# Expert stage of a two-block transformer kernel: tokens of an expert group gathered once, pair by pair after

## The reference

```python
def hier_moe(h, w_grp, b_grp, w_exp, b_exp, w1, w3, w2):
    """Top-1 group routing then top-2 expert routing within the group; SwiGLU experts."""
    ...
    grp_p = jax.nn.softmax(tf @ w_grp.astype(f32) + b_grp.astype(f32), axis=-1)
    g_idx = jnp.argmax(grp_p, axis=-1)
    ...
    top_p, top_i = lax.top_k(jax.nn.softmax(in_grp, axis=-1), TOP_K)
    ...
        hid = jax.nn.silu(xb @ w1[e]) * (xb @ w3[e])
        return (hid @ w2[e]) * w_b[:, None].astype(t.dtype)
```

## Time and profile before

| | us |
|---|---|
| median of 3 runs (lowest to highest) | 2380.0 (2376.22 to 2380.07) |
| the profiled execution | 2379.42 |
| its span in the trace | 2377.5 |
| TensorE busy in it | 2333.4 (98%) |
| VectorE (DVE) busy | 970.1 (41%) |
| ScalarE (ACT) busy | 430.5 (18%) |

### The profile page before, as it was taken

How to read it: one execution, slowest core, us unless ns; L and a number is a source line. 1 busy time by engine, 2 the same in 40 slices (tenths; PEclk the granted TensorE clock), 3 DMA queues, 4 the chain that set the end, 5 groups by cost and what they waited for, 6 DMA issues and landing times.

```text
span 2377.5 us, 24384 instructions
## 1 busy us (share of the span) xinstructions
PE 2333.4 (98%) x10310; PEld 1388.3 (58%) x10310; DVE 970.1 (41%) x1839; ACT 430.5 (18%) x971; POOL 75.3 (3%) x130
## 2 busy tenths in 40 slices
PE   8999999999999999999899999999999999999998
PEld 5568548875586448786444444435878644444443
DVE  3567656677576544462222221222355321122112
ACT  3310003365100021220111111111122021111111
POOL 2000000010100000000000000000000000000000
PEclk9999999999999999999999999999999999999999
DMA  7379625354796342256899999993325589999995
GB/s 283 127 308 394 234 89 190 131 202 165 283 406 258 129 160 102 93 216 244 338 427 428 427 428 428 426 411 123 138 92 228 229 359 427 427 428 428 428 426 238
DMA packets 57434, 671.53 MB, mean 282 GB/s; under 512 B 7312, under 2 KB 7600, under 8 KB 18528
## 3 DMA queue, kind: packets, MB, share of 16 engines
q1 hardware_dynamic: 50160, 649.45, 67.1%
q0 software_dynamic: 7152, 20.39, 2.5%
HBM read 666.56 MB, written 3.26 MB: 282 GB/s over the span
## 4 chain that ended last, share of the span: by engine, by line
PE 93%; DVE 3%; DMA 3%; ACT 0%; issue 0%; POOL 0%; SPq 0%; DVEq 0%; POOLq 0%; ACTq 0%
PE ps L101 91%; DMA ring<-in_mlp_w 1%; DVE arena L117 1%; DVE arena L114 1%; DMA arena<-ssm_rows 1%; PE ps L323 1%; PE ps L2465 1%; DMA ring<-in_attn_w_in 1%; PE ps L2447 0%; PE ps L593 0%; DVE X L117 0%; PE ps L1722 0%; DVE arena L110 0%; ACT arena L106 0%; PE ps L1184 0%
## 5 line engine op out<-in xcount | busy, mean ns | idle before, releaser
L101 PE MATMUL ps<-arena 128*64 128x512 f32 (+5 forms) x3656 | 864.2, 462 | 5.8 <-DVE arena L117 3.7
L101 PEld LDWEIGHTS ps<-arena 128*128 128x128 f32 (+2 forms) x3656 | 418.0, 168 | 370.0 <-issue 351.8
L101 PE MATMUL ps<-XTGB,ring 128*128 128x256 f32 x2544 | 565.7, 381 | 5.0 <-DMA ring<-in_mlp_w 5.0
L101 PE MATMUL ps<-ring,arena 128*64 128x512 f32 (+1 forms) x1808 | 555.0, 593 | 0.0
L101 PEld LDWEIGHTS ps<-XTGB,ring 128*128 128x128 f32 x2544 | 479.9, 190 | 78.9 <-issue 7.8
L101 PEld LDWEIGHTS ps<-ring,arena 128*64 128x64 f32 (+1 forms) x1808 | 195.7, 149 | 284.9 <-issue 282.5
L117 DVE TENSOR_TENSOR arena<-ps,arena 128x512 f32<-128x512 f32 (+4 forms) x166 | 96.0, 613 | 364.8 <-PE ps L101 351.4
L101 PE MATMUL ps<-ring,XTGB 128*128 128x512 f32 (+3 forms) x568 | 226.6, 557 | 1.6 <-DMA ring<-in_attn_w_in 1.0
L101 PE MATMUL ps<-XTGB,arena 128*64 128x512 f32 (+1 forms) x576 | 197.6, 499 | 0.0
L121 ACT COPY arena<-ps 128x512 f32<-128x512 f32 (+2 forms) x169 | 75.7, 469 | 601.1 <-PE ps L101 279.5
L117 DVE TENSOR_TENSOR arena<-arena,ps 128x512 f32<-128x512 f32 x36 | 24.8, 688 | 388.6 <-PE ps L101 388.6
(11 more groups left out here) (140 smaller groups left out, 924.0 us busy)
## 6 DMA issues: line engine op xcount, KB each, us to landing
ring<-in_exp_w SPq DMA_DIRECT2D x88, 2048.0 KB, 19.6
arena<-in_exp_w SPq DMA_DIRECT2D x80, 2048.0 KB, 18.7
ring<-in_mlp_w SPq DMA_DIRECT2D x26, 2048.0 KB, 8.9
XTGB<-in_exp_w SPq DMA_DIRECT2D x20, 2048.0 KB, 19.4
ring<-in_ada_w SPq DMA_DIRECT2D x19, 2048.0 KB, 10.1
ring<-in_ssm_w_in SPq DMA_DIRECT2D x12, 2048.0 KB, 7.8
ring<-in_w_in SPq DMA_DIRECT2D x12, 2048.0 KB, 7.8
ring<-in_gate_w SPq DMA_DIRECT2D x12, 2048.0 KB, 7.8
```

What stands on the lines that cost most here:

```text
L101: return self.e.matmul(o, lhsT=lhsT, rhs=rhs, start=start, stop=stop, skip_group_check=True)
```

## The change

The first thing that the stage does now is to give each token a place in its group: a small pair of matmuls (`grank`) on the group mask, then `gcode` and `pg`, a matrix of 256 tokens x 128 places of the group. `group_rows(g)` brings the group's tokens together as up to 128 rows `xr` with four matmuls of 512 columns. `group_cols` does the same with the group's eight columns of `code` and of `wc`; they go to `cs`. From then on a pair's psel is one tile of 128x128 (group places x pair places), the gather reads xr with one matmul for each column block, `turn_w` is one transpose, and `combine` is one matmul for each half of the columns, which adds the four pairs of a group up in two PSUM banks (`ys`) held for the whole stage. After a group's last pair, DVE multiplies the sum by the gate (`group_sum`), `scatter(g)` brings it back to the tokens with four matmuls through `pgt` (pg turned), and DVE adds the four results to X (`to_tokens`). `rows_out` is a plain copy. psel has one buffer instead of two. The flag is also set if a group has more than 128 tokens.

Where the new steps stand on TensorE: grank, group_rows(0), rank, group_cols for code, then the first gather; `turn_g` between exp_w1 and exp_w3 of the second pair of a group; group_rows and both group_cols of the next group between exp_w1 and exp_w3 of the fourth; scatter of the group before ahead of the outer product of the first. The copies of xr are on ACT.

```diff
-            ps = bank(pe, "rank", l, hold=True)
-            pe.wait_ge(at("msk", l))
-            pe.mm(ps[:, 0:64], C["lt"], msk.rearrange("p t e -> p (t e)"), True, False)
-            pe.then_inc(pe.mm(ps[:, 32:64], C["ones"], msk[:, 0, :], False, True), ("rank", l))
+            ps = bank(pe, "grank", l)
+            pe.wait_ge(at("gm", l))
+            pe.mm(ps[:, 0:8], C["lt"], gm.rearrange("p t g -> p (t g)"), True, False)
+            pe.then_inc(pe.mm(ps[:, 4:8], C["ones"], gm[:, 0, :], False, True), ("grank", l))
+            def group_rows(g):
+                pe.wait_ge(at("pg", l, g))
+                for n in range(2):
+                    ps = bank(pe, "xr", l, g, n)
+                    for t in range(2):
+                        ins = pe.mm(ps, pg[:, t, :], H2[:, t, n * 512:(n + 1) * 512], t == 0, t == 1)
+                    pe.then_inc(ins, ("xr", l, g, n))
+            def group_cols(g, name, x):
+                ps = bank(pe, name, l, g)
+                pe.wait_ge(at("code" if name == "gc" else "wc", l))
+                for t in range(2):
+                    ins = pe.mm(ps[:, 0:8], pg[:, t, :], x[:, t, 8 * g:8 * g + 8], t == 0, t == 1)
+                pe.then_inc(ins, (name, l, g))
+            def turn_g(g):
+                ps = bank(pe, "pgt", l, g)
+                for t in range(2):
+                    ins = pe.e.transpose(ps[:, t * P:(t + 1) * P], pg[:, t, :], C["ident"])
+                pe.then_inc(ins, ("pgt", l, g))
             def gather(i, c0):
-                pe.wait_ge(at("psel", l, i))
+                pe.wait_ge(at("psel", l, i), at("xr ready", l, i // 4, c0 // 4))
                 ps = bank(pe, "xg", l, i, c0)
                 for c in range(c0, c0 + 4):
-                    for t in range(2):
-                        ins = pe.mm(ps[:, (c - c0) * P:(c - c0 + 1) * P], H2[:, t, c * P:(c + 1) * P],
-                                    psel[i % 2][:, t, :], t == 0, t == 1)
+                    ins = pe.mm(ps[:, (c - c0) * P:(c - c0 + 1) * P], xr[:, c * P:(c + 1) * P], psel, True, True)
                 pe.then_inc(ins, ("xg", l, i, c0))
             def turn_w(i):
                 ps = bank(pe, "pw", l, i)
                 pe.wait_ge(at("pw", l, i))
-                for t in range(2):
-                    ins = pe.e.transpose(ps[:, t * P:(t + 1) * P], pw[:, t, :], C["ident"])
-                pe.then_inc(ins, ("pwt", l, i))
+                pe.then_inc(pe.e.transpose(ps[:, 0:P], pw, C["ident"]), ("pwt", l, i))
...
             def combine(i, n):
+                g = i // 4
+                if i % 4 == 0 and g:
+                    pe.wait_ge(at("yg", l, g - 1, n))
                 pe.wait_ge(at("pwt ready", l, i), at("xy ready", l, i, n))
-                for t in range(2):
-                    ps = bank(pe, "xc", l, i, t, n)
-                    pe.then_inc(pe.mm(ps, pwt[i % 2][:, t * P:(t + 1) * P], x_y[:, n * 512:(n + 1) * 512],
-                                      True, True), ("xc", l, i, t, n))
+                pe.then_inc(pe.mm(ys[n], pwt[i % 2], x_y[:, n * 512:(n + 1) * 512], i % 4 == 0, i % 4 == 3),
+                            ("xc", l, i, n))
+            def scatter(g):
+                for n in range(2):
+                    pe.wait_ge(at("pgt ready", l, g), at("yg", l, g, n))
+                    for t in range(2):
+                        ps = bank(pe, "xo", l, g, t, n)
+                        pe.then_inc(pe.mm(ps, pgt[:, t * P:(t + 1) * P], x_y[:, n * 512:(n + 1) * 512], True, True),
+                                    ("xo", l, g, t, n))
+            rank = bank(pe, "rank", l, hold=True)
+            group_rows(0)
+            pe.wait_ge(at("msk", l))
+            pe.mm(rank[:, 0:64], C["lt"], msk.rearrange("p t e -> p (t e)"), True, False)
+            pe.then_inc(pe.mm(rank[:, 32:64], C["ones"], msk[:, 0, :], False, True), ("rank", l))
+            group_cols(0, "gc", code)
             for c0 in (0, 4):
                 gather(0, c0)
-            for t in range(2):
-                ins = pe.mm(ps[:, 64:96], C["ones"], msk[:, t, :], t == 0, t == 1)
+            for x, o in ((msk, slice(64, 96)), (gm, slice(96, 100))):
+                for t in range(2):
+                    ins = pe.mm(rank[:, o], C["ones"], x[:, t, :], t == 0, t == 1)
             pe.then_inc(ins, ("counts", l))
             banks.drop(("rank", l))
+            ys = [bank(pe, "ys", l, n, hold=True) for n in range(2)]
             for i in range(NP):
                 inner(i, "exp_w1")
                 if i == 0:
-                    turn_w(0)
-                if i == 1:
+                    group_cols(0, "gw", wc)
+                elif i == 1:
                     reg = flag_reg(pe, l)
+                if i % 4 == 1:
+                    turn_g(i // 4)
+                elif i % 4 == 3 and i + 1 < NP:
+                    group_rows(i // 4 + 1)
+                    group_cols(i // 4 + 1, "gc", code)
+                    group_cols(i // 4 + 1, "gw", wc)
                 inner(i, "exp_w3")
                 if i >= 1:
                     combine(i - 1, 0)
                 else:
+                    turn_w(0)
                     gather(1, 0)
                 turn_h(i)
                 if i >= 1:
...
                     gather(i + 1, 4)
                 if i + 1 < NP:
                     turn_w(i + 1)
+                if i % 4 == 0 and i:
+                    scatter(i // 4 - 1)
                 outer(i)
             for n in range(2):
                 combine(NP - 1, n)
+            scatter(NG - 1)
+            for n in range(2):
+                banks.drop(("ys", l, n))
...
+            def group_rows(g):
+                for n in range(2):
+                    act.wait_ge(at("xr", l, g, n))
+                    if g:
+                        act.wait_ge(at("xg", l, 4 * g - 1, 4))
+                    act.then_inc(act.cp(xr[:, n * 512:(n + 1) * 512], ps_of("xr", l, g, n)), ("xr ready", l, g, n),
+                                 ("read", "xr", l, g, n))
+            group_rows(0)
...
+                if i % 4 == 3 and i + 1 < NP:
+                    group_rows(i // 4 + 1)
...
+            def groups():
+                v.wait_ge(at("grank", l), at("gm", l))
+                v.then_inc(v.stt(gcode, ps_of("grank", l)[:, 0:8].rearrange("p (t g) -> p t g", t=2), 1.0, gm, ALU.add,
+                                 ALU.mult), ("gcode", l), ("read", "grank", l))
+            def group_places(g):
+                v.wait_ge(at("gcode", l))
+                if g:
+                    v.wait_ge(at("xr", l, g - 1, 1), at("gc", l, g - 1), at("gw", l, g - 1), at("pgt", l, g - 1))
+                v.then_inc(v.tt(pg, C["iota"].unsqueeze(1).to_broadcast([P, 2, P]),
+                                gcode[:, :, g:g + 1].to_broadcast([P, 2, P]), ALU.is_equal), ("pg", l, g))
+            def group_cols(g, name, o):
+                v.wait_ge(at(name, l, g))
+                v.then_inc(v.cp(cs[:, o:o + 8], ps_of(name, l, g)[:, 0:8]), (name + " in", l, g), ("read", name, l, g))
+            def group_turned(g):
+                v.wait_ge(at("pgt", l, g))
+                if g:
+                    v.wait_ge(at("xo", l, g - 1, 1, 1))
+                v.then_inc(v.cp(pgt, ps_of("pgt", l, g)[:, 0:T]), ("pgt ready", l, g), ("read", "pgt", l, g))
+            k = best(lg[:, :, 0:4], 4, 1, gm, at("lg", l), ("gm", l))
             v.wait_ge(k)
             k = v.then_inc(v.tt(four(tm), four(lg[:, :, 4:36]), per_group(gm), ALU.mult))
             v.wait_ge(k)
             k = v.then_inc(v.red(sel, tm.rearrange("p t (g e) -> p t e g", g=4), ALU.add))
+            groups()
+            group_places(0)
...
             def places(i):
-                v.wait_ge(at("code", l))
-                if i >= 2:
-                    v.wait_ge(at("xg", l, i - 2, 4))
-                v.then_inc(v.tt(psel[i % 2].rearrange("p t (e s) -> p t e s", e=2),
-                                C["iota"].unsqueeze(1).unsqueeze(1).to_broadcast([P, 2, 2, CAP]),
-                                code[:, :, 2 * i:2 * i + 2].unsqueeze(3).to_broadcast([P, 2, 2, CAP]),
-                                ALU.is_equal), ("psel", l, i))
+                j = 2 * (i % 4)
+                v.wait_ge(at("gc in", l, i // 4))
+                if i >= 1:
+                    v.wait_ge(at("xg", l, i - 1, 4), at("pw", l, i - 1))
+                v.then_inc(v.tt(psel.rearrange("p (e s) -> p e s", e=2),
+                                C["iota"][:, 0:CAP].unsqueeze(1).to_broadcast([P, 2, CAP]),
+                                cs[:, j:j + 2].unsqueeze(2).to_broadcast([P, 2, CAP]), ALU.is_equal), ("psel", l, i))
             def weigh(i):
-                v.wait_ge(at("psel", l, i), at("wc", l))
+                j = 8 + 2 * (i % 4)
+                v.wait_ge(at("psel", l, i), at("gw in", l, i // 4))
                 if i >= 1:
                     v.wait_ge(at("pwt", l, i - 1))
-                v.then_inc(v.tt(pw.rearrange("p t (e s) -> p t e s", e=2),
```

(72 more changed lines are left out.)

45 lines of the change are left out of this document (27 added, 18 removed).

## The result

The changed kernel takes 2384.35 us (median of 14 runs, 2380.61 to 2388.05) against 2379.43 us for the kernel before in the same rounds (14 runs, 2376.22 to 2381.25). The ratio is 1.0022, 95% interval 1.0015 to 1.0030: slower by 0.2%, 4.9 us. The prediction said 2385, and slower as the likeliest of the three. The profiled execution took 2384.8 us, its span is 2383.0, 5.5 us longer than before.

What follows compares the result with a forecast made beforehand. It took slab transfers, 0.9 us a pair slower than TensorE, to end the expert stage once their lead is gone. Terms -5.1 + 1.8 + 4.8 + 1.4 = +2.9 us a layer, +5.8 on 2379.4: 2385, range 2375 to 2395.

Steps and rivals of the forecast that it cites:

- the lead of the transfers: Expert stage: nine slabs of lead at its start; would shrink 2.4 us a pair and be gone near pair 9.
- start, gm to release: Stage start, group mask to tenth slab's release: new steps and half clock delay all later slabs, +4.8 us a layer.
- release to the last exp_w3 product: End of stage: pair 15's exp_w3 starts when its slab lands, 1577.0 instead of 1580.4, -3.4 us a layer.
- its end to the last xy: Behind the last exp_w3: one combine matmul instead of two on each side of turn_h, less waits, -1.7 us a layer.
- slow clock in it: Last pair: idle of about 4 us before the last exp_w3 slows the clock, 0 to 3.4 us, taken as +1.4.
- tail: After the last xy: a combine matmul and the GATE[5] multiplication stand before the first scatter matmul, +1.8 us a layer.
- the step of ACT's queue: Stage start: copy of xr queued behind Exp of ex, so gather can start at 1145.0 at the earliest.
- rival (c): TensorE: clock falls at every wait, start +7 and end +3.4, +7.1 us a layer: 2393.6; chance 0.20.
- (a): Expert stage: TensorE keeps the pace and its 48 us saving counts in full: 2332; chance 0.05.
- (b): Bound by DMA but quick start and full clock, -2.4 us a layer: 2374.6, up to 2380; chance 0.20.
- (d): The change does not do what it says: overfull-expert path runs above 128 tokens a group; no price, hardly a chance.
- the queue was never empty: Transfers from the release at 1153.80 on: queue always full, so last slabs land when they did before.

Runs made afterwards that it cites:

- The half loads: Every expert weight slab loaded only in its first half: the kernel before 2380.3 us, ratio 1.0002; the changed kernel 2337.67 us, ratio 0.9821.
- the kernel of shorter gathers: The kernel before, with the gather of pairs 1 to 15 reading only the first half of the tokens, 8 matmuls instead of 16: 2371.72 us, ratio 0.9972.
- the order on ACT: The changed kernel with the first group's two copies of xr ahead of Exp of ex on ACT instead of behind it: 2376.8 us, ratio 0.9986.
- the fillers: The changed kernel with xr's copies ahead of Exp, plus three unread matmuls of 360 columns ahead of grank: 2373.37 us, ratio 0.9972.
- the kernel with the end filled: The changed kernel with three unread matmuls of 512 columns ahead of each layer's last exp_w3 product: 2377.5 us, ratio 0.9991.
- the filler ahead of the gather: The changed kernel with three unread matmuls of 360 columns between group_cols and the first gather: 2381.01 us, ratio 1.0012 to the kernel before.
- the early release: The changed kernel with xr's copies ahead of Exp, tenth and eleventh slabs in four parts, first released after a quarter of pair 0's exp_w1 product: 2376.07 us, ratio 0.9988.

## Why the prediction was right

*What bounds the kernel.* Right, and the step that carried the case: the lead of the transfers shrinks and the rest of the saving is lost. The half loads show both sides of it. TensorE's waits for slabs begin at 1369.5, in pair 8, where pair 9 was named, and with three short waits of about 1 us that the profile puts down to issue they come to 16.7 us in the first layer; 2.4 us a pair from pair 9 on makes 17.

*The four terms*, as the profiled executions have them, first and second layer:

| term | predicted | first layer | second layer |
|---|---|---|---|
| start, gm to release | +4.8 | +2.4 | +8.8 |
| release to the last exp_w3 product | -3.4 | -4.7 | -4.7 |
| its end to the last xy | -1.7 | -1.6 | -1.6 |
| slow clock in it | +1.4 | +1.7 | +1.6 |
| tail | +1.8 | +1.9 | +1.9 |
| sum | +2.9 | -0.3 | +6.0 |

The sum of both is +5.7 and the span grew by 5.5; predicted were +5.8. The second row is 421.9 us (1155.89 to 1577.79) against 426.6 (1153.80 to 1580.4): 3.4 us of it are the lead, as predicted, and 1.3 come from transfers that took that much less in this execution. The third is 9.5 us against 11.2, the fifth 4.67 (2367.57 to 2372.24) against 2.76, the same in both layers.

That the sum met the measured time to less than 1 us is partly luck. The two starts cost 11.2 us more where 9.6 were predicted, and the transfers gave back 2.6 us that were not predicted; these two misses offset each other, and another execution can have another second start.

*The start* was right as a mean and wrong as a picture: I took one value for both layers, and they differ by 6.4 us. In the first, the clock was back at full before the gather, as I assumed in part. In the second it was at half until 1908, came back to 1.00 (1909.5 to 1911) and fell again in the idle of 1.84 us behind Exp and the copies and stayed low through gather and product (3.75 and 9.27 us instead of 2.02 and 7.09), which was the end of my range, +7, and beyond. Against the chain that I had laid out, the step of ACT's queue was the one that mattered most: it costs 1.25 us a layer by itself and opens the idle. The moved copy was cheap to see in the program and worth more than the whole loss, 7.6 us against 4.9.

*The clock at the end.* Right in place and size: 8.78 us for the product, 7.09 with the idle filled. The rule of the Trainium skill, "TensorE: Matmul & The Clock Gate", section "HAM oscillation — how this bites in real kernels", that waits for DMA between groups of matmuls throw the clock back, was borne out by the trace in this place: behind the wait of 2.76 us the clock was 0.55. That it happens at every wait, as in rival (c), was not: of the five waits of over 1 us for weights ahead of the last one in the first layer, one was followed by a fall (2.75 us, up to 1430.7), while one of 2.76 us, up to 1548.4, was not. The second layer repeats it: 0.51 behind 2.74 us (up to 2202.4), 1.00 behind 2.76 us (up to 2319.9). The windows of the first layer behind these two waits (columns as in the earlier trace rows, the clock third from the end):

```profile
1430.50:1433.50 3.00, 2.76 (x8) 1.14 (x10) 0.00 (x0) 0.00 (x0) 0.00 (x0) 0.59 1.01 431
1548.40:1552.00 3.60, 3.58 (x18) 1.55 (x20) 0.00 (x0) 0.00 (x0) 0.00 (x0) 1.00 1.02 437
```

*The rivals.* (a), TensorE keeps the pace, has fallen with the kernel of shorter gathers: 2371.7 where that theory gives 2328. (b), a quick start at full clock, is what the order on ACT and the fillers make of the kernel: 2376.8 and 2373.4, against its 2374.6. (c) is the second layer's start. (d) was not tested by a run; the timeline shows the stage's usual products throughout and nothing of the general path.

*One sentence of it went too far*, "the queue was never empty" from the release on. For the kernel before and the changed one it holds, but only since pair 0's next releases just keep up with it; when the first came earlier, the second one was the gap, and an experiment was misjudged by 9 us for it.

## What to carry to other kernels

Before an engine's work is cut, ask how far the other stream is behind it: compare issue and landing of a slab early and late in the stage; if landings drift away from issues while the queue is full, the gain ends when the lead is used up. In such a stage only three things count: when the queue can restart (the first release, and every one after it until the queue is full), how much work stands behind the last landing, and how fast the queue moves. Then look at what a new step waits for on an engine that seemed to be off the path: here one Exp ahead of a copy decided between slower and faster.

## What the runs showed of the hardware

The clock's fall behind a short idle was not the same from one execution to another. The same 1.84 us ahead of the gather was followed by 0.57 from 1911 to 1923 in the changed kernel's profile and by a product of 7.09 us at full clock in that of the kernel with the end filled. The changed kernel's runs spread over 7.4 us, those of the kernel before over 5.0, and its time goes with the mean granted clock of the run: the three runs at 0.991 took 2380.6 to 2383.2 us, the five at 0.989 or 0.988 took 2384.8 to 2388.1. How often the second layer's start falls was not measured, so the split of the 4.9 us between the longer path and the clock stays open: with the order on ACT the two go together (7.6 us), the filler ahead of the gather alone took 3.3.

Ahead of the last exp_w3 product the same holds within one execution. In the kernel before with less TensorE work an idle of 2.30 us in the first layer was followed by a slow product, one of 2.29 us in the second by a fast one:

```profile
1575.93 8.71 PE L101 MATMUL ps<-ring,arena 128*64 128x512 f32 x32 [2.30 <-DMA ring<-in_exp_w]
...
2337.89 7.09 PE L101 MATMUL ps<-ring,arena 128*64 128x512 f32 x32 [2.29 <-DMA ring<-in_exp_w]
```

Over the profiles of the seven kernels in which TensorE waits for whole last exp_w3 slabs and has no fillers ahead of them, two layers each, the product took 8.7 to 8.8 us in all seven layers with an idle of 2.43 to 2.76 us, and in two of the seven with 2.29 to 2.40 us; in the other five it took 7.09. So some of the differences between two runs of this document hold 1.7 us of clock a layer that their edits did not cause.

Useless matmuls in a wait of 2 to 3 us cost nothing that could be measured. In the profiles of the four kernels that have them the clock behind them was full in seven cases of eight: ahead of the gather in two layers, ahead of grank in three of four, ahead of the last product in two. In both second layers with fillers ahead of grank the clock was down before they began (their six records took 3.95 and 3.76 us, in the first layers 2.06); behind them group_rows took 5.42 us in one and 3.70 in the other.

In the first microseconds behind a release the queue is slow whatever the size of the parts: 256 GB/s in the changed kernel with whole slabs of 16 KB a partition (1155.9 to 1160), 233 with parts of 4 KB (1152 to 1157, the early release). Behind that the parts moved 329 and 401 GB/s (1157 to 1160 and to 1163), whole slabs 431 (1160 to 1163). Whether the size of the parts or a queue that is short of work made this difference is not separated.
